# A state-space scan stage: forget-gate sums moved behind a tile's last products, the last output products moved inside the next unit, the last result moved between the forget-gate scans

## The chip, the cores and the metric

The kernel runs on one core of one Trainium2 chip. The metric is the time of one execution on the device in microseconds (us); the value given is the median of several runs. The engines are named as in the profile: PE (TensorE), DVE (VectorE), ACT (ScalarE), POOL (GpSimd) and SP (the queue that issues the weight loads).

## The reference, cut to what matters

The whole computation is a two-block network on one sequence of 512 positions and width 1024, followed by a second block. The second block mixes three branches of the same normalised input: an attention branch, a state-space branch (S5) and a gated linear recurrence (HGRN2). The change touches the S5 branch, the first steps of the HGRN2 branch and the first products of the merge.

```python
# S5: a complex linear recurrence over the 512 positions, 32 groups of 64 states
_, _, h_r, h_i = lax.associative_scan(_complex_linear_combine, elems, axis=1)
y = (jnp.einsum('bsgp,ghp->bsgh', h_r, c_re) - jnp.einsum('bsgp,ghp->bsgh', h_i, c_im))
y = y.reshape(bsz, seq, S5_W) + d_skip * uf
z = jax.nn.gelu(y)
out = z * jax.nn.sigmoid(z @ w_glu + b_glu)

# HGRN2: the log of the forget gate, and its running sum inside a chunk
log_f = jnp.logaddexp(jnp.log(lb), jnp.log1p(-lb) + jax.nn.log_sigmoid(z))
b = jnp.cumsum(lfc, axis=2)

# merge
merged = (gates[:, :, 0] * (y_fox @ wb[:BRANCH_W]) + gates[:, :, 1] * (y_s5 @ wb[BRANCH_W:2 * BRANCH_W])
          + gates[:, :, 2] * (y_hg @ wb[2 * BRANCH_W:]))
```

## The kernel before, in words

Every weight passes through a ring of four slots: SP loads a unit of 128x1024 into `w_stage`, ACT copies its high part to `w_hi`, POOL subtracts to get the low part `w_lo`, and PE multiplies three times for each block (high by high, high by low, low by high, lines 460 to 462). A unit is 24 such products of 128x512.

The S5 stage treats 16 tiles `t` of 128 states. All engines have their own written-out instruction order, and only semaphores tie them. For each tile, PE makes the drive (`drive(t)`, lines 2041 and 2042, into banks 4 and 5). DVE multiplies it by sine and cosine (lines 2130 to 2139, six instructions), scans it along the sequence (lines 2151 and 2153), and makes two products of the imaginary part (lines 2157 and 2158, the tile's last products, semaphore `s5_nprod`). POOL makes two products of the real part (lines 2087 and 2088) and then two additions that join both (line 2092, semaphore `s5_sum`). PE multiplies the sums by the output weights (`outputs(t)`, line 2032, into bank 7, semaphore `s5_ymm`). Since a tile uses the same banks as the one before it, `drive(t)` waits until `s5_nprod` says that the last products of tile `t-1` are made.

Between these steps, PE works through 17 units of other weights: first half of unit `u`, `outputs(u-2)`, second half, `drive(u)`. Units 0 to 11 are projections for HGRN2, whose result DVE takes from the bank (`take`, line 2115), 12 to 15 another projection that ACT takes, and unit 16 is the first of the merge. After unit 16 comes `outputs(15)`, and then the merge goes on in `pe_hg` with the gate `pe_merge_gate(pe, 0, 2, 1)` (the second unit of the merge), a branch (third unit), and the gate of the next triple (fourth unit).

DVE has more work in this loop: `dve_hg_forget_sum` (line 2794) makes for two heads each, in tiles 6 and 8, the log of the forget gate from `hq` and one of `ss` and `hf_odd`. Both operands are in SBUF. `s5_result` (line 2168) takes four tiles' outputs from bank 7; it waits for `s5_ymm`. It runs after tiles 4, 8 and 12, and the fourth time after the loop and after `dve_hg_forget_scan` (line 2801, `ones` and `hq`, both in SBUF; 16 instructions, 4 for each of 4 heads). The fourth result is what ACT's last GELU waits for (line 2242); behind it in ACT's order stand four copies (line 2245) and then `w_hi` of the merge's fourth unit (line 424), which POOL's `w_lo` of that unit (line 455) waits for. DVE goes on with a memset (line 2164), four subtractions for the low part of the GELU (`dve_z`, line 2250, `su` and `y_hi`, both in SBUF) and the scaling of the merge's first gate (line 2296).

The wait of a merge gate on PE names both its weights and its bank:

```python
pe.wait_ge(w_lo_ready, L.base + u + i + 1)
pe.wait_ge(taken, L.rbase + r + i + 1 - RING)
```

For the merge's fourth unit the second line means the first line-2296 instruction: DVE must have taken the first gate from bank 0.

Of the kernel before, what the change touches and what calls it, by code (L numbers as in the profile page):

```python
# [24 lines left out]
KD = D // P  # L25
# [66 lines left out]
def build(nc, io):  # L92
# [1899 lines left out]
    def pe_s5(pe):  # L1992
        QFG, V, M = layers["hg_qfg"], layers["hg_v"], layers["merge01"]

        def first_half(u):
            if u < 12:
                pe.wait_ge(w_lo_ready, QFG.base + u + 1)
                pe.wait_ge(taken, QFG.rbase if u in (1, 2) else QFG.rbase + u + 1 - RING)
            elif u == 16:
                pe.wait_ge(w_lo_ready, M.base + 1)  # L2000
                pe.wait_ge(taken, M.rbase + 1 - RING)
            else:
                pe.wait_ge(w_lo_ready, V.base + u - 12 + 1)
            half(u, 0)

        def half(u, part):

            if 12 <= u < 16:
                k = 2 * (u - 12) + part
                wh, wl = (w[:, u % RING, part * T:(part + 1) * T] for w in (w_hi, w_lo))  # L2010
                for t in range(4):
                    if k == 0:
                        pe.wait_ge(taken, V.rbase)
                    c = slice(t * P, (t + 1) * P)
                    pe.matmul(bank[t][:], xg_hi[:, k, c], wh, start=k == 0, stop=False)
                    pe.matmul(bank[t][:], xg_lo[:, k, c], wh, start=False, stop=False)
                    mm = pe.matmul(bank[t][:], xg_hi[:, k, c], wl, start=False, stop=k == KD - 1)
            else:
                for k in range(4 * part, 4 * part + 4):
                    mm = three_passes(pe, s5_unit_bank(u)[:], u % RING, k, xg_hi[:, k, :], xg_lo[:, k, :], k == 0, k == KD - 1)  # L2020
            if part:
                mm.then_inc(unit_used, 1)

        def outputs(t):

            j = 32 * (t % 4)
            out = bank[7][j:j + 32, :]
            if t >= 4 and t % 4 == 0:
                pe.wait_ge(s5_y, t // 4)
            for c, product in enumerate((gbuf[:], sq[:, 0, :])):  # L2030
                pe.wait_ge(s5_sum, 2 * t + c + 1)
                mm = pe.matmul(out, s5_cx[:, c, t, :], product, start=c == 0, stop=c == 1)  # L2032
            mm.then_inc(s5_ymm, 1)

        def drive(t):
            j, jr = 32 * (t % 4), (32 * (t % 4) + 32) % P
            if t >= 1:
                pe.wait_ge(s5_nprod, 2 * t)
            if t % 4 == 0:
                pe.wait_ge(su_turned, 32 * (t // 4 + 1))  # L2040
            pe.matmul(bank[4][:], s5_bt[j:j + 32, 0, t // 4, :], su[j:j + 32, t // 4, :], start=True, stop=True)  # L2041
            pe.matmul(bank[5][:], s5_bt[jr:jr + 32, 1, t // 4, :], su_r[t // 4 % 2][jr:jr + 32, :],
                      start=True, stop=True).then_inc(s5_drive, 1)

        pe.wait_ge(s5_bt_ready, 2)
        pe.wait_ge(att_exp, FOX_STEPS - 2)
        drive(0)
        pe.wait_ge(s5_turn, 1)
        first_half(0)
        pe_fox_transposes(pe, SLOTS - 1, 0)  # L2050
        pe_fox_outputs(pe, SLOTS - 2)
        pe_fox_transposes(pe, SLOTS - 1, 1)
        half(0, 1)
        pe_fox_outputs(pe, SLOTS - 1)
        pe.wait_ge(s5_cx_ready, 4)
        for u in range(1, 17):
            if u == 3:
                pe.wait_ge(fox_lo, 4)
            first_half(u)
            if u >= 2:  # L2060
                outputs(u - 2)
            half(u, 1)
            if u < 16:
                drive(u)
        outputs(15)

    def s5_unit_bank(u):
        return bank[0 if u == 16 else (u + 2) % RING]
# [41 lines left out]
    def dve_s5(dve):  # L2110
        QFG, V = layers["hg_qfg"], layers["hg_v"]

        def take(t):
            dve.wait_ge(unit_used, QFG.base + t + 1)
            dve.tensor_tensor(hq[:, QFG_TILE[t], :], s5_unit_bank(t)[:], rstd[:], ALU.mult).then_inc(taken, 1)

        for t in range(16):
            if 1 <= t < 12:
                take(t)
            if 1 <= t < 15:  # L2120
                dve_s5_fraction(dve, t + 1)
            if t == 1:
                dve.wait_ge(levels_ready, 1)
            sin, cos, gr = s5_state(t)
            dr, di, m0, m1 = bank[4][:], bank[5][:], s5_m[:, 0, :], s5_m[:, 1, :]
            n0 = 8 * t
            dve.wait_ge(s5_rot, 3 * t + 3)
            dve.wait_ge(s5_drive, t + 1)

            dve.tensor_tensor(m0, dr, sin, ALU.mult).then_inc(s5_step, 1)  # L2130
            dve.tensor_tensor(m1, di, sin, ALU.mult).then_inc(s5_step, 1)
            dve.wait_ge(s5_step, n0 + 1)
            dve.tensor_tensor(dr, dr, cos, ALU.mult).then_inc(s5_step, 1)
            dve.wait_ge(s5_step, n0 + 2)
            dve.tensor_tensor(di, di, cos, ALU.mult).then_inc(s5_step, 1)
            dve.wait_ge(s5_step, n0 + 3)
            dve.tensor_tensor(dr, dr, m1, ALU.add).then_inc(s5_step, 1)
            dve.wait_ge(s5_step, n0 + 4)
            dve.tensor_tensor(di, di, m0, ALU.subtract).then_inc(s5_step, 1)
            if t == 0:  # L2140
                take(0)
                dve_fox_low(dve, 3)
                dve_s5_fraction(dve, 1)
            if t in (6, 8):
                dve_hg_forget_sum(dve, t - 6)
                dve_hg_forget_sum(dve, t - 5)
            mag = s5p[:, 3, t:t + 1].to_broadcast([P, T])
            if t >= 2:
                dve.wait_ge(s5_prod, 2 * t - 2)
            dve.wait_ge(s5_step, n0 + 5)  # L2150
            dve.tensor_tensor_scan(gr, mag, dr, 0.0, ALU.mult, ALU.add).then_inc(s5_step, 1)
            dve.wait_ge(s5_step, n0 + 6)
            dve.tensor_tensor_scan(di, mag, di, 0.0, ALU.mult, ALU.add).then_inc(s5_step, 1)
            if t >= 1:
                dve.wait_ge(s5_sum, 2 * t)
            dve.wait_ge(s5_step, n0 + 8)
            dve.scalar_tensor_tensor(ubuf[:], di, -1.0, sin, ALU.mult, ALU.mult).then_inc(s5_nprod, 1)
            dve.tensor_tensor(sq[:, 1, :], di, cos, ALU.mult).then_inc(s5_nprod, 1)
            if t % 4 == 0 and t:
                s5_result(dve, t // 4 - 1)  # L2160
        for h in range(HEADS):
            dve_hg_forget_scan(dve, h)
        s5_result(dve, 3)
        dve.memset(hsc, 0.0).then_inc(hg_zero, 1)

    def s5_result(dve, i):
# [623 lines left out]
    def dve_hg_forget_sum(dve, h):  # L2790

        dve.wait_ge(hg_key, HEADS)
        dve.wait_ge(hg_ln, h + 1)
        dve.scalar_tensor_tensor(hg_b(h), hg_b(h), 0.0, hg_logf(h), ALU.min, ALU.subtract).then_inc(hg_min, 1)
# [241 lines left out]
            act_merge_gate(act, *unit)  # L3036

    def pe_hg(pe):
        pe_merge_gate(pe, 0, 2, 1)
        pe_merge_branch(pe, 0, 2)  # L3040
        pe_triple(pe, 0, 3)
        pe_glu(pe)
        for h in range(HEADS):
            pe_share(pe, share(h, 0))
            if h:
                pe_hg_out(pe, h - 1)
            pe_hg_scores(pe, h, 0)
            pe_hg_scores(pe, h, 1)
            if h:
                pe_hg_sum(pe, h - 1)  # L3050
            pe_share(pe, share(h, 1))
            pe_hg_scores(pe, h, 2)
            pe_hg_scores(pe, h, 3)
            if h:
                pe_hg_spread(pe, h - 1)
            pe_share(pe, share(h, 2))
            pe_hg_scores(pe, h, 4)
            pe_hg_scores(pe, h, 5)
            pe_share(pe, share(h, 3))
            pe_hg_scores(pe, h, 6)  # L3060
            pe_hg_keys(pe, h)
            pe_hg_scores(pe, h, KD_STEP)
            pe_share(pe, share(h, 4))
            pe_hg_update(pe, h)
        pe_merge_gate(pe, 2, 0, 0, (0, 1, 2, 3, 4))
        pe_hg_out(pe, HEADS - 1)
        pe_merge_gate(pe, 2, 0, 0, (5, 6))
        pe_hg_sum(pe, HEADS - 1)
        pe_merge_gate(pe, 2, 0, 0, (7,))
        pe_merge_gate(pe, 2, 0, 1, (0, 1))  # L3070
        pe_hg_spread(pe, HEADS - 1)
        pe_merge_gate(pe, 2, 0, 1, (2, 3, 4, 5, 6, 7))
# [383 lines left out]
```

## Time and profile before

| | us |
|---|---|
| median of 3 runs (lowest, highest) | 2835.97 (2835.58, 2836.41) |
| the profiled execution: its own time | 2836.24 |
| its span in the trace | 2834.5 |
| PE busy in the span | 2801.3 |

The profiled execution was 0.27 us above the median, and 1.7 us of its time lie around the span. Times of rows count from the span's start. Consecutive DVE instructions overlap a little in the trace: one of 0.69 us is followed by the next after 0.60 us, so that costs are read from start to start.

### The profile page before, as it was taken

To read this page: it belongs to the slowest core of one execution; us is meant where nothing else is said; L and a number is where in the kernel's file an instruction comes from. 1 tells how busy PE (TensorE), PEld (TensorE's weight loads), DVE (VectorE), ACT (ScalarE), POOL (GpSimd) and SP (SyncE) were. 2 spreads that over 40 slices of the span, in tenths; PEclk is the share of its full clock that TensorE was granted. 3 is DMA by queue.
4 is the path that set the end of the run, shared out by engine and by line. 5 is a ranking of instruction groups with operands and counts; after the bars stand their busy time and mean duration, and the time that the engine had idled before them with its cause. 6 is when DMAs were issued, how large, how long until landed. Compare 5 with 4: busy or idle time off the path is not lost.

```text
span 2834.5 us, 45729 instructions
## 1 busy us (share of the span) xinstructions
PE 2801.3 (99%) x16460; PEld 2399.2 (85%) x16460; DVE 1652.0 (58%) x2696; ACT 1346.6 (48%) x2076; POOL 1570.8 (55%) x872
## 2 busy tenths in 40 slices
PE   7999999999999999999999999999999999999999
PEld 6998877899889998888999886765688888799987
DVE  6777147577616774135777416589788363467730
ACT  5554256555525554243555333566444344455531
POOL 5775445677546774443777443158633373377743
PEclk9999999999999999999999999999999999999999
DMA  3223322222332233332223332112222242122332
GB/s 136 104 104 113 104 82 82 90 104 104 104 102 92 104 107 106 99 110 84 90 104 122 99 105 71 48 50 67 82 75 75 97 148 75 52 93 109 111 102 76
DMA packets 80684, 267.89 MB, mean 95 GB/s; under 512 B 11168, under 2 KB 13216, under 8 KB 80560
## 3 DMA queue, kind: packets, MB, share of 16 engines
q1 hardware_dynamic: 77904, 262.01, 27.7%
q10 hardware_dynamic: 2656, 4.26, 0.5%
q8 instruction: 73, 1.20, 0.2%
q14 instruction: 51, 0.42, 0.0%
HBM read 263.09 MB, written 2.10 MB: 94 GB/s over the span
## 4 chain that ended last, share of the span: by engine, by line
PE 93%; DVE 4%; ACT 2%; issue 1%; DMA 0%; POOL 0%; ACTq 0%; SPq 0%; DVEq 0%
PE bank L460 17%; PE bank L461 17%; PE bank L462 17%; PE bank L701 10%; PE bank L703 10%; PE bank L702 10%; PE bank L532 1%; PE bank L534 1%; PE bank L533 1%; PE bank L1620 1%; PE bank L2032 1%; PE bank L2894 1%; PE bank L2630 0%; PE bank L2041 0%; PE bank L2610 0%
## 5 line engine op out<-in xcount | busy, mean ns | idle before, releaser
L448 POOL TENSOR_TENSOR w_lo<-w_stage,w_hi 128x1024 fp32r<-128x1024 f32 (+1 forms) x228 | 533.8, 2347 | 729.8 <-ACT w_hi L424 729.3
L424 ACT ACTIVATE w_hi<-w_stage 128x1024 fp32r<-128x1024 f32 (+1 forms) x412 | 421.1, 1027 | 367.9 <-PE bank L462 301.1
L788 POOL TENSOR_TENSOR w_lo<-w_stage,w_hi 128x1024 fp32r<-128x1024 f32 (+1 forms) x176 | 327.2, 1859 | 201.8 <-ACT w_hi L424 201.8
L460 PE MATMUL bank<-xg_hi,w_hi 128*128 128x512 f32 x976 | 395.9, 406 | 7.9 <-DVE h_raw L1048 6.4
L455 POOL TENSOR_TENSOR w_lo<-w_stage,w_hi 128x1024 fp32r<-128x1024 f32 (+1 forms) x96 | 235.9, 2462 | 263.4 <-ACT w_hi L424 218.9
L461 PE MATMUL bank<-xg_lo,w_hi 128*128 128x512 f32 x976 | 381.1, 390 | 0.0
L462 PE MATMUL bank<-xg_hi,w_lo 128*128 128x512 f32 x976 | 381.0, 390 | 0.0
L460 PE MATMUL bank<-h_hi,w_hi 128*128 128x512 f32 x880 | 342.3, 389 | 0.0
L461 PE MATMUL bank<-h_lo,w_hi 128*128 128x512 f32 x880 | 342.3, 389 | 0.0
L462 PE MATMUL bank<-h_hi,w_lo 128*128 128x512 f32 x880 | 342.3, 389 | 0.0
L703 PE MATMUL bank<-xg_hi,w_lo 128*128 128x256 f32 x1056 | 299.2, 283 | 0.0
L701 PE MATMUL bank<-xg_hi,w_hi 128*128 128x256 f32 x1056 | 298.9, 283 | 0.0
L702 PE MATMUL bank<-xg_lo,w_hi 128*128 128x256 f32 x1056 | 298.8, 283 | 0.0
L701 PE MATMUL bank<-xsum,s_w 128*128 128x256 f32 x1056 | 296.1, 280 | 0.0
L703 PE MATMUL bank<-xsum,s_w 128*128 128x256 f32 x1056 | 294.6, 279 | 0.0
L702 PE MATMUL bank<-xsum,s_w 128*128 128x256 f32 x1056 | 294.6, 279 | 0.0
L1121 DVE SCALAR_TENSOR_TENSOR x_res<-bank,x_res 128x512 f32 x64 | 44.0, 688 | 408.2 <-PE bank L462 408.2
L460 PEld LDWEIGHTS bank<-xg_hi,w_hi 128*128 128x128 f32 x976 | 183.6, 188 | 76.1 <-issue 37.2
L1013 DVE TENSOR_TENSOR s_w<-bank,s_w 128x512 fp32r<-128x512 f32 x176 | 121.7, 692 | 190.3 <-ACT s_w L918 190.3
L461 PEld LDWEIGHTS bank<-xg_lo,w_hi 128*128 128x128 f32 x976 | 183.8, 188 | 40.4 <-issue 4.6
L462 PEld LDWEIGHTS bank<-xg_hi,w_lo 128*128 128x128 f32 x976 | 183.5, 188 | 39.6
L701 PEld LDWEIGHTS bank<-xg_hi,w_hi 128*128 128x128 f32 x1056 | 202.4, 192 | 0.2
(526 smaller groups left out, 6610.5 us busy)
## 6 DMA issues: line engine op xcount, KB each, us to landing
w_stage<-w_up SPq DMA_DIRECT2D x220, 512.0 KB, 4.2
w_stage<-w_down SPq DMA_DIRECT2D x80, 512.0 KB, 3.5
w_stage<-merge SPq DMA_DIRECT2D x36, 512.0 KB, 3.4
w_stage<-w_down SPq DMA_DIRECT2D x40, 384.0 KB, 3.1
w_stage<-hg_qfg SPq DMA_DIRECT2D x12, 512.0 KB, 3.4
w_stage<-rec_r SPq DMA_DIRECT2D x8, 512.0 KB, 3.4
w_stage<-rec_y SPq DMA_DIRECT2D x8, 512.0 KB, 3.5
w_stage<-rec_out SPq DMA_DIRECT2D x8, 512.0 KB, 3.4
```

What stands on the lines that cost most here:

```text
L424: act.activation(w_hi[:, r, 0:w], w_stage[:, r, 0:w], ACT.Copy).then_inc(w_hi_ready, 1)
L448: pool.tensor_tensor(w_lo[:, r, 0:w], w_stage[:, r, 0:w], f32(w_hi[:, r, 0:w]), ALU.subtract).then_inc(w_lo_ready, 1)
L455: pool.tensor_tensor(w_lo[:, r, 0:w], w_stage[:, r, 0:w], f32(w_hi[:, r, 0:w]), ALU.subtract).then_inc(w_lo_ready, 1)
L460: pe.matmul(out, w_hi[:, r, c], hi, start=start, stop=False)
L461: pe.matmul(out, w_hi[:, r, c], lo, start=False, stop=False)
L462: return pe.matmul(out, w_lo[:, r, c], hi, start=False, stop=stop)
L701: pe.matmul(out, wh[:, c], xh[:, k, :], start=k == 0, stop=False)
L702: pe.matmul(out, wh[:, c], xl[:, k, :], start=False, stop=False)
L703: mm = pe.matmul(out, wl[:, c], xh[:, k, :], start=False, stop=k == 3)
L788: pool.tensor_tensor(w_lo[:, r, cs], w_stage[:, r, cs], f32(w_hi[:, r, cs]), ALU.subtract).then_inc(w_lo_ready, 1)
L1013: dve.tensor_tensor(lo, src[:], f32(hi), ALU.subtract).then_inc(wsum_lo_ready, 1)
L1121: dve.scalar_tensor_tensor(tile(x, m), bank[mm % 4][:], scale, tile(x, m), ALU.mult, ALU.add).then_inc(taken, 1)
```

## The change

Three edits. On DVE, the forget-gate sums of tiles 6 and 8 are issued behind that tile's last products instead of ahead of its scans. On PE, the first four of the eight blocks of the gate that follows unit 16 are issued ahead of `outputs(15)` and the other four behind it; the call in `pe_hg` goes. On DVE, the fourth result is issued after the scans of two heads instead of after those of four.

```diff
             if u < 16:
                 drive(u)
+        pe_merge_gate(pe, 0, 2, 1, range(4))
         outputs(15)
+        pe_merge_gate(pe, 0, 2, 1, range(4, KD))
...
-            if t in (6, 8):
-                dve_hg_forget_sum(dve, t - 6)
-                dve_hg_forget_sum(dve, t - 5)
             mag = s5p[:, 3, t:t + 1].to_broadcast([P, T])
...
             dve.tensor_tensor(sq[:, 1, :], di, cos, ALU.mult).then_inc(s5_nprod, 1)
+            if t in (6, 8):
+                dve_hg_forget_sum(dve, t - 6)
+                dve_hg_forget_sum(dve, t - 5)
             if t % 4 == 0 and t:
                 s5_result(dve, t // 4 - 1)
         for h in range(HEADS):
+            if h == 2:
+                s5_result(dve, 3)
             dve_hg_forget_scan(dve, h)
-        s5_result(dve, 3)
         dve.memset(hsc, 0.0).then_inc(hg_zero, 1)
...
     def pe_hg(pe):
-        pe_merge_gate(pe, 0, 2, 1)
         pe_merge_branch(pe, 0, 2)
```

DVE in tile 8, before: the sums (line 2794) stand ahead of the scans (lines 2151 and 2153), and the result (line 2168) follows the last product.

```order
L2139 TENSOR_TENSOR bank<-bank,s_m 128x512
L2794 SCALAR_TENSOR_TENSOR hq<-hq,ss 128x512
L2794 SCALAR_TENSOR_TENSOR hq<-hq,hf_odd 128x512
L2151 SCALAR_TENSOR_TENSOR s_g_136<-s5p,bank 128x512
L2153 SCALAR_TENSOR_TENSOR bank<-s5p,bank 128x512
L2157 SCALAR_TENSOR_TENSOR ubuf<-bank,rot 128x512
L2158 TENSOR_TENSOR sq<-bank,rot 128x512
L2168 SCALAR_TENSOR_TENSOR su<-su,par,bank 128x512
L2115 TENSOR_TENSOR hq<-bank,rstd 128x512
```

The same stretch of DVE in the changed kernel (its line 2797 is the sum, 2171 the result, 2117 the take):

```order
L2141 TENSOR_TENSOR bank<-bank,s_m 128x512
L2150 SCALAR_TENSOR_TENSOR s_g_136<-s5p,bank 128x512
L2152 SCALAR_TENSOR_TENSOR bank<-s5p,bank 128x512
L2156 SCALAR_TENSOR_TENSOR ubuf<-bank,rot 128x512
L2157 TENSOR_TENSOR sq<-bank,rot 128x512
L2797 SCALAR_TENSOR_TENSOR hq<-hq,ss 128x512
L2797 SCALAR_TENSOR_TENSOR hq<-hq,hf_odd 128x512
L2171 SCALAR_TENSOR_TENSOR su<-su,par,bank 128x512
L2117 TENSOR_TENSOR hq<-bank,rstd 128x512
```

The two sums now stand behind the tile's last product, directly ahead of the result and the take; tile 6 is the same without the result.

DVE behind the last tile in the changed kernel (line 2804 is the forget-gate scan, 2253 the subtraction of `dve_z`, 2299 the scaling of the gates):

```order
L2157 TENSOR_TENSOR sq<-bank,rot 128x512
L2804 SCALAR_TENSOR_TENSOR hq<-ones,hq 128x128 x8
L2171 SCALAR_TENSOR_TENSOR su<-su,par,bank 128x512
L2804 SCALAR_TENSOR_TENSOR hq<-ones,hq 128x128 x8
L2167 MEMSET sq 128x512
L2253 TENSOR_TENSOR y_lo<-su,y_hi 128x512 x4
L2299 TENSOR_TENSOR gbuf<-bank,rstd 128x512
```

Before, all 16 scans stood ahead of the result. Eight of them moved behind it.

## Rows read from the trace of the kernel before

**Rows 1.** The page: busy time of each engine over the span.

```profile
PE 2801.3 (99%) x16460; PEld 2399.2 (85%) x16460; DVE 1652.0 (58%) x2696; ACT 1346.6 (48%) x2076; POOL 1570.8 (55%) x872
```

**Rows 2.** Waits of PE from 1860 to 2100 us: total, times, longest.

```profile
PE bank L2041 <- DVE sq L2158: 2.1, 3, 1.0
PE bank L2032 <- POOL gbuf L2092: 1.2, 1, 1.2
PE bank L460 <- POOL w_lo L455: 1.2, 1, 1.2
```

**Rows 3.** Timeline of DVE, tiles 6 to 8: start, duration, instruction.

```profile
1919.21 0.69 DVE L2130 TENSOR_TENSOR s_m<-bank,rot 128x512 f32<-128x512 f32 x1
...
1922.81 0.68 DVE L2794 SCALAR_TENSOR_TENSOR hq<-hq,ss 128x512 f32<-128x512 f32 x1
...
1924.01 1.21 DVE L2151 TENSOR_TENSOR_SCAN s_g<-s5p,bank 128x512 f32<-128x512 f32 x1
...
1927.65 0.68 DVE L2115 TENSOR_TENSOR hq<-bank,rstd 128x512 f32<-128x512 f32 x1
...
1929.03 0.69 DVE L2130 TENSOR_TENSOR s_m<-bank,rot 128x512 f32<-128x512 f32 x1
...
1946.37 0.74 DVE L2168 SCALAR_TENSOR_TENSOR su<-su,par,bank 128x512 f32<-128x512 f32 x1
1947.03 0.68 DVE L2115 TENSOR_TENSOR hq<-bank,rstd 128x512 f32<-128x512 f32 x1
```

**Rows 4.** Timeline of PE: the drives of tiles 7, 8 and 10.

```profile
1927.79 0.69 PE L2041 MATMUL bank<-su,s_bt 32*128 32x512 f32 x1 [0.91 <-DVE sq L2158]
...
1936.63 0.69 PE L2041 MATMUL bank<-su,s_bt 32*128 32x512 f32 x1
...
1955.59 0.69 PE L2041 MATMUL bank<-su,s_bt 32*128 32x512 f32 x1 [0.18 <-DVE sq L2158]
```

**Rows 5.** Timeline of POOL in tile 6.

```profile
1920.47 2.41 POOL L455 TENSOR_TENSOR w_lo<-w_stage,w_hi 128x1024 fp32r<-128x1024 f32 x1
1925.30 1.30 POOL L2087 TENSOR_TENSOR gbuf<-s_g,rot 128x512 f32<-128x512 f32 x1 [2.42 <-DVE s_g L2151]
1926.55 1.28 POOL L2088 TENSOR_TENSOR sq<-s_g,rot 128x512 f32<-128x512 f32 x1
1927.79 1.27 POOL L2092 TENSOR_TENSOR gbuf<-gbuf,ubuf 128x512 f32<-128x512 f32 x1
```

**Rows 6.** Line 2801 and line 2454: duration min/median/max, first and last start.

```profile
L2801 DVE TENSOR_TENSOR_SCAN hq<-ones,hq x16: 393/394/2522, 2008.2 to 2017.2; 128x128 f32<-128x128 f32 x16
...
L2454 DVE SCALAR_TENSOR_TENSOR m_lo<-merged,m_hi x8: 678/2873/2878, 2286.7 to 2300.4; 128x512 fp32r<-128x512 f32 x8
```

**Rows 7.** Timelines of DVE and POOL behind the last tile.

```profile
2008.19 0.47 DVE L2801 TENSOR_TENSOR_SCAN hq<-ones,hq 128x128 f32<-128x128 f32 x1
2008.59 1.41 DVE L2801 TENSOR_TENSOR_SCAN hq<-ones,hq 128x128 f32<-128x128 f32 x1
...
2008.34 1.38 POOL L2092 TENSOR_TENSOR gbuf<-gbuf,ubuf 128x512 f32<-128x512 f32 x1
...
2011.02 2.49 POOL L455 TENSOR_TENSOR w_lo<-w_stage,w_hi 128x1024 fp32r<-128x1024 f32 x1
```

**Rows 8.** Scans of line 2801 in one stretch: length, DVE busy (count), clock, DMA.

```profile
2013.60:2017.50 3.90, 3.90 (x13) 1.00 0.19 69
```

**Rows 9.** Timelines of DVE, POOL and PE, from the fourth result to the merge's fourth unit.

```profile
2017.49 0.72 DVE L2168 SCALAR_TENSOR_TENSOR su<-su,par,bank 128x512 f32<-128x512 f32 x1
...
2019.43 2.50 DVE L2250 TENSOR_TENSOR y_lo<-su,y_hi 128x512 fp32r<-128x512 f32 x4 [0.68 <-ACT y_hi L2245]
2021.85 0.68 DVE L2296 TENSOR_TENSOR gbuf<-bank,rstd 128x512 f32<-128x512 f32 x1
...
2021.99 2.38 POOL L455 TENSOR_TENSOR w_lo<-w_stage,w_hi 128x1024 fp32r<-128x1024 f32 x1 [8.49 <-ACT w_hi L424]
...
2012.09 0.50 PE L460 MATMUL bank<-xg_hi,w_hi 128*128 128x512 f32 x1
...
2024.43 0.50 PE L460 MATMUL bank<-xg_hi,w_hi 128*128 128x512 f32 x1 [1.17 <-POOL w_lo L455]
```

## The prediction, made before the changed kernel ran

> **What bounds the kernel now.** I read the page first: PE is busy in 2801.3 of 2834.5 us [rows 1], so that only what PE waits for, some 33 us in all, can be gained. Then I read PE's waits in the stretch that the change touches. There are three kinds: three waits of drives for a tile's last products on DVE, 2.1 us together, one wait of the last output products for POOL's sums, 1.2 us, and one of the merge's fourth unit for its low weights, 1.2 us [rows 2]. The change aims at all of them, and all of them together are 4.5 us, 0.16% of the time. 0.2% of it, 5.7 us, is about what a measurement of this kernel can tell from no change. So the first answer is that even a full success is hardly measurable; the rest of the text asks for the sign.
>
> The timelines then show how tight the loop is. From the drive of tile 7 to that of tile 8 PE takes 8.84 us with no wait [rows 4]. DVE's part of this round is: the first multiplication starts 1.24 us after the drive (1927.79 to 1929.03) [rows 3, 4]; from there to the end of the last product are 7.24 us (1919.21 to 1927.65, less 1.20 for the two sums that lie between) [rows 3]; PE follows that end by 0.14 us (1927.65 to 1927.79) [rows 3, 4]. Together 8.62, so a tile has 0.22 us to spare, and whatever DVE is given in addition comes out as a wait of a drive, whether it stands ahead of the scans or behind the products. Position changes only what it meets.
>
> **The sums.** Two instructions in tile 6 and two in tile 8. Where they stand now, each pair costs 1.20 us (1922.81 to 1924.01) [rows 3]. POOL is idle in that time: its `w_lo` ends at 1922.9 and its next product waits for DVE's scan until 1925.30 [rows 5]. Behind the products it is different. Without the sums ahead of the scans, POOL's second product runs from 1925.35, and its first sum begins at 1926.59 (1926.55 and 1927.79, less 1.20) [rows 5], and POOL goes on without a pause for two sums and a `w_lo`. DVE's last product ends at 1926.45. So the moved pair falls between POOL instructions that stand back to back.
>
> What this costs I read where it already happens, behind tile 15, where the scans of line 2801 take the very place that the sums get. The first is issued 0.15 us ahead of POOL's sum at 2008.34 and passes; the second is issued at 2008.59 and lasts 1.41 us, as long as POOL's instruction, in place of the usual 0.39 [rows 6, 7]. The longest is 2.52 us, beside a `w_lo` of 2.49 [rows 6, 7]. Line 2454, a 128x512 instruction of the sum's form with both inputs in SBUF, has a median of 2.87 us where it runs beside `w_lo` and 0.68 at least [rows 6]. The instructions of the S5 tile itself, which have one input in PSUM, are not stretched beside the same POOL instructions (0.69 and 0.68 in tile 6 to 8) [rows 3]. I read: one DVE instruction with two SBUF inputs passes between two of POOL's, and the next waits one whole POOL instruction.
>
> The Trainium skill says this of the port pair that VectorE and GpSimd share (SBUF — State Buffer, Who interferes with whom): a VectorE instruction with two SBUF inputs and a GpSimd instruction that reads SBUF exclude each other, and the later one blocks until the earlier is done. By that rule the moved sums lose time; by the sums' own rows alone (0.68 each) they would win a little. The trace agrees with the rule, with 0.39 against 1.41 us.
>
> Tile 6 by that: the first sum waits from 1926.45 to 1926.59 and takes about 0.5; POOL's sum, 1.25 us, goes ahead of the second, until 1928.35; the second ends at 1928.85. Take and the next fraction are 1.20 (two at 0.60), the first multiplication of tile 7 starts at 1930.05, its last product ends 7.24 later at 1937.29, and drive 8 starts at 1937.43, against 1936.63 before [rows 4]: 0.80 later. (PE would be free for it at about 1935.7: 1927.79 less the wait of 0.91, and 8.84 [rows 4].) Tile 8: the first multiplication at 1938.67, last product 1945.91, drive 9 without a wait at 1946.27. The pair costs 2.40 again, to 1948.31, and now the result of 0.66 us (1946.37 to 1947.03) [rows 3] stands behind it, to 1948.97; take and fraction 1.20, 1950.17; last product 1957.41, drive 10 at 1957.55 against 1955.59 [rows 4]. From there on the rounds are as before. **Sums: 1.95 us lost.** Bounds: 0.45 gained if nothing collides (the same chain with 1.20 in place of 2.40 gives drive 10 at 1955.14, since DVE's short pause ahead of the take is used), 4.5 lost if each pair meets one more POOL instruction of 1.25. I take the middle, since the phase of 0.14 us is that of tile 15, which has been seen.
>
> **The end of the stage**, in times of the trace before, without the shift of 1.95. PE has no wait behind unit 16: 12 products, at 0.23 us each 2.8 us ((2024.43 less 1.17 less 2012.09) by 48) [rows 9], run while POOL makes the sums. The wait of 1.2 for the first sum, and one of 0.3 for the second, go. The weights and the bank of that gate are ready, since POOL's `w_lo` of this unit is made two instructions ahead of the products of tile 15. The output products end at about 2013.4 in place of 2012.1. The second half of the gate follows, and PE wants the fourth unit at 2024.43 less the waits of 1.17, 1.2 and 0.3, which is 2021.8.
>
> Does it get it? The scans go through at one to each POOL instruction until the `w_lo` of 2011.02 is over; the other 12 take 3.90 us, 0.325 each (the row counts one of the waiting ones too) [rows 7, 8]. So the first eight are done at 2017.49 less 2.6, 2014.9, behind the output products: the result starts there with no wait and 2.6 us earlier than now. ACT and then POOL follow as before 4.50 us after it (2017.49 to 2021.99) [rows 9]: `w_lo` at 2019.4, its own 2.4, ready at 2021.8. That is just in time.
>
> But the fourth unit also needs the first gate taken. DVE is behind the result at 2015.55, behind the other scans at 2018.15, behind the memset at 2018.75 (result to line 2250 is 1.94 with a wait of 0.68 in it, so 0.6 for the memset) [rows 9]. Now the four line-2250 subtractions start, 0.605 each [rows 9], both inputs in SBUF, and POOL's `w_lo` falls at 2019.4 into the middle of them; before, it started at 2021.99, 0.14 us after the last [rows 9]. It holds DVE up by some 2.3 us. Line 2296 starts at 2023.4 in place of 2021.85, ends at 2024.1, and PE starts the fourth unit at 2024.15, against 2024.43. **End of the stage: 0.3 us gained.** Bounds: nothing if DVE is held for 2.6 us, 2.5 gained if the subtractions are not held (line 2296 at 2021.2, PE at 2021.9). I take the collision, since both starts follow from chains seen in the rows and they fall well inside each other.
>
> From there on PE has nothing to wait for until DVE's work on the scores, which itself starts when PE ends the next branch; DVE idles twice for over 4 us before it, so that lateness of a microsecond on DVE or ACT is absorbed, and the shift is carried to the end.
>
> **The sum.** 1.95 less 0.3 is 1.65 us lost. The profiled execution would go from 2836.24 to 2837.9; the median from 2835.97 to 2837.6.
>
> **Rivals.**
> *No collisions.* DVE and POOL do not hold each other in the new places: sums gain 0.45, the end gains 2.5, the time is 2833.0. For it speaks only that the sums are 0.68 us long now; against it the stretched rows [rows 6]. 10%. Only the sums free, the subtractions held: 2835.2, 4%.
> *The sums collide, the subtractions don't* (ACT's chain is later, or POOL waits): 1.95 less 2.5, the time is 2835.4. 12%.
> *Slower: the sums miss the gap.* The first sum passes only because DVE asks 0.14 us ahead of POOL's sum. If DVE's last product ends more than 0.14 us later relative to POOL, each pair meets two POOL sums and costs 1.25 more, twice: 2.5, the time is 2840.1. Tile 15 shows the gap met once, which speaks against. 8%.
> *The wait at the new result.* If the output products ended later than 2014.9, DVE's other scans would stand behind the wait; each 1 us beyond would be 1 us at the fourth unit. By the rows there are 1.5 us to spare. 3%.
>
> **How the numbers follow.** The forecast of 2837.6 has 63%; its own range is 2836.6 to 2838.6, from the 0.1 to 0.3 us that each of the four collisions is uncertain. The range of 2834.0 to 2839.5 adds the second rival and the half-collision and the smaller forms of the others, and leaves out the first and the third. All cases are within 0.2% of 2835.97 (2830.3 to 2841.6), so "same" has 95%; 2% and 3% are left for what I have not seen on either side.
>
> **What the changed profile would show.** Line 2797: two short and two long ones, 1.4 to 1.9 us, in place of four at 0.68. Drives: 8 and 10 wait, 1.8 and 2.4 us, 7 and 9 don't. No wait at line 2032 for POOL. The result starts 6.7 us after DVE's last product in place of 9.3. One line-2253 subtraction of 2.5 to 3 us. At the merge's fourth unit a wait of some 2.4 us for line 2299 and not for `w_lo`. I am wrong if line 2797 stays at 0.68, or if PE's waits in this stretch sum to less than 4.5 us.

## The result and the profile after

The changed kernel is slower: median 2845.71 us (2837.16 to 2849.76, 7 runs) against 2835.83 (2832.78 to 2838.14, 7 runs), ratio 1.0033, 95% interval 1.0024 to 1.0043. The forecast was 1.65 us more; it is nearly 10. The profiled execution took 2849.76 us with a span of 2847.9.

The steps that were forecast are there, at their places and nearly at their sizes. PE's waits over the whole span of the changed kernel, longest sums first (total, times, longest):

```profile
PE bank L486 <- ACT xg_hi L3244: 8.3, 1, 8.3
PE bank L460 <- DVE h_raw L1048: 4.3, 1, 4.3
PE bank L2041 <- DVE sq L2157: 4.0, 2, 2.3
PE bank L460 <- DVE yh_lo L1267: 2.7, 6, 0.8
PE bank L460 <- DVE gbuf L2299: 2.5, 1, 2.5
```

The drives' waits are 4.0 us in place of 2.1, the wait of the output products for POOL is gone, and the merge's fourth unit waits 2.5 us for line 2299 and no longer 1.2 for its low weights [rows 2]. Within the touched stretch this is 6.5 us of waits in place of 4.8 (0.3 of the second sum with it), 1.7 us more, which is what the prediction had.

The moved sums, DVE and POOL in tile 6 of the changed kernel (timelines: start, duration, instruction):

```profile
1928.54 0.68 DVE L2157 TENSOR_TENSOR sq<-bank,rot 128x512 f32<-128x512 f32 x1
1929.14 0.76 DVE L2797 SCALAR_TENSOR_TENSOR hq<-hq,ss 128x512 f32<-128x512 f32 x1
1929.82 1.75 DVE L2797 SCALAR_TENSOR_TENSOR hq<-hq,hf_odd 128x512 f32<-128x512 f32 x1
1931.50 0.68 DVE L2117 TENSOR_TENSOR hq<-bank,rstd 128x512 f32<-128x512 f32 x1
...
1928.04 1.31 POOL L2090 TENSOR_TENSOR sq<-s_g,rot 128x512 f32<-128x512 f32 x1
1929.30 1.73 POOL L2094 TENSOR_TENSOR gbuf<-gbuf,ubuf 128x512 f32<-128x512 f32 x1
1930.99 1.74 POOL L2094 TENSOR_TENSOR sq<-sq 128x512 f32<-128x512 f32 x1
```

The first sum passes between two POOL instructions, the second waits for one. The pair takes 2.36 us (1929.14 to 1931.50) where it took 1.20 [rows 3]. POOL pays as well: its sums take 1.73 us where one took 1.27 [rows 5], since each stands behind a DVE instruction. This agrees with the Trainium skill on the shared port (SBUF — State Buffer, Who interferes with whom). The rows also give the order: in each of these three cases the instruction that waits goes next.

The drives of tiles 8 and 10, on PE:

```profile
1940.06 0.69 PE L2041 MATMUL bank<-su,s_bt 32*128 32x512 f32 x1 [1.69 <-DVE sq L2157]
...
1960.12 1.01 PE L2041 MATMUL bank<-su,s_bt 32*128 32x512 f32 x1 [2.35 <-DVE sq L2157]
```

They wait 1.69 and 2.35 us; 1.8 and 2.4 were forecast. But the second one is 1.01 us long where it was 0.69 [rows 4]. That is the first sign of what was not forecast. The end of the stage, on DVE and POOL:

```profile
2022.66 0.71 DVE L2171 SCALAR_TENSOR_TENSOR su<-su,par,bank 128x512 f32<-128x512 f32 x1
2023.30 2.62 DVE L2804 TENSOR_TENSOR_SCAN hq<-ones,hq 128x128 f32<-128x128 f32 x8
2025.98 0.48 DVE L2167 MEMSET sq<- 128x512 f32 x1
2026.38 4.61 DVE L2253 TENSOR_TENSOR y_lo<-su,y_hi 128x512 fp32r<-128x512 f32 x4
2030.91 0.68 DVE L2299 TENSOR_TENSOR gbuf<-bank,rstd 128x512 f32<-128x512 f32 x1
...
2027.16 2.69 POOL L455 TENSOR_TENSOR w_lo<-w_stage,w_hi 128x1024 fp32r<-128x1024 f32 x1 [5.96 <-ACT w_hi L424]
```

The four subtractions take 4.61 us where they took 2.50 [rows 9], because the low weights now fall into them. PE starts the merge's fourth unit at 2031.74, with a wait of 2.50. From DVE's end of tile 15 that is 15.9 us (2015.85 to 2031.74), where it was 16.2 (2008.19 to 2024.43) [rows 7, 9]: 0.35 gained, 0.3 forecast.

So where are the other 8 us? The page gives PE 2816.7 us busy in place of 2801.3 [rows 1], with the same instructions: PE did the same work more slowly. (The profiled execution is 13.5 us longer than that of before: 15.4 us of slower work and the 1.7 us of waits, less 3.3 us by which the first two waits of the kernel, 8.3 and 4.3 us here, are shorter than before's 9.5 and 6.4, at the start and far from the change, and 0.3 us elsewhere.) Stretches around the wait of drive 10, around that of the fourth unit, and one ahead of the whole change (stretch: length, busy and count of PE, PEld, DVE, ACT and POOL, then granted clock, DMA share and GB/s):

```profile
1957.00:1958.00 1.00, 0.77 (x4) 0.29 (x2) 1.00 (x2) 0.81 (x1) 0.37 (x1) 1.00 0.74 225
1958.00:1960.00 2.00, 0.00 (x0) 0.00 (x0) 1.90 (x4) 0.00 (x0) 2.00 (x2) 1.00 0.14 49
1960.00:1961.00 1.00, 0.89 (x4) 0.31 (x4) 1.00 (x3) 0.00 (x0) 1.00 (x2) 0.68 0.00 0
1961.00:1967.00 6.00, 6.00 (x16) 3.80 (x12) 5.15 (x9) 4.52 (x7) 3.91 (x3) 0.50 0.16 53
1967.00:1968.00 1.00, 1.00 (x3) 0.25 (x3) 1.00 (x1) 0.00 (x0) 0.00 (x0) 0.91 0.54 217
...
2030.00:2031.00 1.00, 0.00 (x0) 0.00 (x0) 1.00 (x3) 0.00 (x0) 0.00 (x0) 1.00 0.07 18
2031.00:2032.00 1.00, 0.26 (x1) 0.29 (x2) 1.00 (x2) 0.37 (x1) 0.00 (x0) 1.00 0.72 227
2032.00:2035.00 3.00, 3.00 (x8) 2.30 (x8) 2.12 (x4) 2.98 (x5) 1.72 (x1) 0.51 0.02 5
...
1759.00:1769.00 10.00, 10.00 (x29) 6.22 (x26) 5.13 (x14) 3.61 (x10) 2.37 (x2) 0.50 0.05 7
```

Right behind each of the two long pauses the granted clock falls from 2.4 to 1.2 GHz, 0.50 in the column, for some 6.8 and 3.4 us. Sixteen products are made in six microseconds where the kernel before, at the full clock, makes 22 or 23 behind the same drive. The third stretch, 10 us at half clock, ends 160 us ahead of the first instruction that the change moved, behind a pause of only 0.46. Two more, near 2271 and 2441 us, follow no long pause either. The trace of before has none between 50 and 2800 us. Half clock behind 50 us costs this execution 15.4 us in all, 5.1 of them behind the two long pauses and 10.2 at the three other places. One trace each doesn't tell what of this the change did; that was the question for the experiments.

### The profile page after: what moved, and what is told of

The parts are those of the page before. It is cut to its first block, busy times and chain, and to the rows that moved or that the text cites. A ratio compares the mean times of both kernels' runs of the same rounds, so it can differ in the third digit from the quotient of the medians.

```text
span 2847.9 us, 45729 instructions
## 1 busy us (share of the span) xinstructions
PE 2816.7 (99%) x16460; PEld 2411.0 (85%) x16460; DVE 1650.1 (58%) x2696; ACT 1348.8 (47%) x2076; POOL 1572.5 (55%) x872
## 4 chain that ended last, share of the span: by engine, by line
PE 92%; DVE 4%; ACT 2%; issue 1%; DMA 0%; ACTq 0%; SPq 0%; DVEq 0%
PE bank L460 17%; PE bank L461 17%; PE bank L462 17%; PE bank L701 10%; PE bank L703 10%; PE bank L702 10%; PE bank L532 1%; PE bank L534 1%; PE bank L533 1%; PE bank L1620 1%; PE bank L2032 1%; PE bank L2897 1%; PE bank L2041 1%; PE bank L2633 0%; PE bank L2613 0%
## 5 line engine op out<-in xcount | busy, mean ns | idle before, releaser
L788 POOL TENSOR_TENSOR w_lo<-w_stage,w_hi 128x1024 fp32r<-128x1024 f32 (+1 forms) x176 | 327.4, 1860 | 203.2 <-ACT w_hi L424 202.9
```

Source lines behind the costliest of these rows:

```text
L788: pool.tensor_tensor(w_lo[:, r, cs], w_stage[:, r, cs], f32(w_hi[:, r, cs]), ALU.subtract).then_inc(w_lo_ready, 1)
```

## The experiments

Each execution comes with its time and its mean granted clock, the latter to three decimals, which alone leaves 1.4 us open in one execution; so means are compared. Two numbers are used: the mean time, and the mean of time times clock, which takes out what the clock cost and leaves work and waits. (If the clock is low while PE pauses anyway, that product takes out a little too much.) The mean time of the changed kernel is uncertain by 0.8 us (one standard error), of the filled ones together by 0.4, of the single runs by 0.4 to 1.5; time times clock by 0.2 to 0.6.

| kernel | executions | mean us | mean clock | time times clock |
|---|---|---|---|---|
| before (on four chips together) | 122 | 2836.2 | 0.9981 | 2830.8 |
| before, run as `control` | 11 | 2835.4 | 0.9985 | 2831.0 |
| changed (first runs, `after_rep`, `after_rep2`) | 30 | 2843.1 | 0.9959 | 2831.6 |
| `sums_only` | 11 | 2839.9 | 0.9976 | 2833.2 |
| `end_only` | 12 | 2838.5 | 0.9969 | 2829.7 |
| `pause2` | 11 | 2839.1 | 0.9976 | 2832.4 |
| `pause4` | 11 | 2842.3 | 0.9968 | 2833.3 |
| `pause8` | 8 | 2844.5 | 0.9969 | 2835.6 |
| `pause8_fill` | 6 | 2844.5 | 0.9972 | 2836.5 |
| `after_fill`, `after_fill2` | 22 | 2838.5 | 0.9978 | 2832.1 |
| `after_zlate` | 12 | 2838.7 | 0.9967 | 2829.2 |
| `end_zlate`, `end_zlate2` | 22 | 2833.9 | 0.9979 | 2828.0 |
| `best` | 11 | 2836.2 | 0.9972 | 2828.2 |

Before's clock was 0.9978 on the chip on which `control`, `sums_only`, `end_only` and `pause4` ran, and 0.9981 to 0.9982 on the three others; against before on their own chip the four took 1.5 us less and 3.0, 1.6 and 5.4 us more.

Two theories stood against each other: P, that the long pauses of PE bring the stretches at half clock, and R, that these belong to the chip or the hour.

**Is the clock the chip's?** The kernel before, run as a kernel of its own.

> The kernel before, unchanged, run as if it were a new one, so that the granted clock of each of its executions is listed. Theory P (the PE pauses that the change made longer bring stretches at half clock): clock 0.998 to 0.999 in nearly all executions, time 2836, no stretch at half clock behind 50 us. Rival R (the stretches belong to the chip or the hour, not to the change, since one of them lies ahead of the first changed instruction): clock 0.993 to 0.998 here too, and single executions up to 2845.

Measured: median 2834.87, ratio 0.9995 (0.9986 to 1.0003), clock 0.997 at the lowest, none of the 11 executions at 0.996 or below; of the changed kernel's 30 it is 20. But its trace isn't clean: it has half-clock time too, near 2260 and 2428 us, 1.7 us lost at each. The first as a stretch of ten microseconds (same columns):

```profile
2260.00:2270.00 10.00, 10.00 (x75) 10.00 (x75) 1.27 (x3) 7.08 (x10) 5.91 (x3) 0.85 0.16 54
```

So such stretches occur in the kernel before as well, a few us an execution, at places that have nothing to do with the change. R holds for those and not, by these 11 executions, for the whole difference.

**The two halves of the change.** First the sums alone behind the products.

```diff
-            if t in (6, 8):
-                dve_hg_forget_sum(dve, t - 6)
-                dve_hg_forget_sum(dve, t - 5)
             mag = s5p[:, 3, t:t + 1].to_broadcast([P, T])
...
+            if t in (6, 8):
+                dve_hg_forget_sum(dve, t - 6)
+                dve_hg_forget_sum(dve, t - 5)
```

> Only the forget-gate sums are moved behind the last products. The waits alone: drives 8 and 10 wait 1.7 and 2.35 us, and the time is 1.9 us longer than before, 2837.7. Theory P: a stretch at half clock of 3 to 7 us behind the wait of 2.35 us in most executions, which costs 1.7 to 3.4 us more, so 2839 to 2841, clock 0.997. Rival R: 2837.7 and a clock as the control's. If the whole clock loss of the changed kernel came from the sums: 2844.

Measured: ratio 1.0011 (1.0002 to 1.0019). The drives wait 4.0 us as in the changed kernel, and the second sums last 1.755 us. Time times clock is 2.4 us above before's; 1.95 was forecast for the waits. No half-clock stretch followed the wait of 2.3 us in its trace, and its clock is as before's within the spread. This run speaks for R.

Then the end of the stage alone: the gate's first half ahead of `outputs(15)` and the result between the scans.

```diff
+        pe_merge_gate(pe, 0, 2, 1, range(4))
         outputs(15)
+        pe_merge_gate(pe, 0, 2, 1, range(4, KD))
...
+            if h == 2:
+                s5_result(dve, 3)
             dve_hg_forget_scan(dve, h)
```

> The sums stay ahead of the scans; the gate's first half goes ahead of the last output products, and the fourth result between the forget-gate scans. The waits alone: one wait of 2.5 us at the merge's fourth unit in place of three of 1.2, 0.3 and 1.2, 0.3 us gained, 2835.5. Theory P: a stretch at half clock behind it, 2837 to 2839. Rival R: 2835.5.

Measured: ratio 1.0006 (0.9997 to 1.0015). The waits are those forecast, and time times clock falls by 1.1 us, more than the 0.3 forecast. The time rises nonetheless: behind the 2.5 us wait the clock is at half. Stretches of this kernel:

```profile
2024.00:2026.00 2.00, 0.17 (x1) 0.00 (x0) 2.00 (x3) 0.00 (x0) 0.77 (x1) 1.00 0.05 9
2026.00:2028.00 2.00, 1.33 (x6) 1.08 (x7) 1.81 (x3) 1.44 (x2) 0.00 (x0) 0.96 0.33 122
2028.00:2030.00 2.00, 2.00 (x6) 1.62 (x5) 1.31 (x2) 1.98 (x4) 1.78 (x1) 0.50 0.00 0
```

Five of its 12 executions have a clock of 0.996 or less, of before's 122 it is 3 in 100. This speaks for P.

**A pause alone.** Nothing of the change; DVE repeats one multiplication of tile 9, so that drive 10 waits longer. `n` is 2, 4 or 8.

```diff
+            for _ in range(n if t == 9 else 0):
+                dve_chain(dve, dve.tensor_tensor(m0, dr, sin, ALU.mult))
             dve.tensor_tensor(m0, dr, sin, ALU.mult).then_inc(s5_step, 1)
```

> The kernel before with four repeats of one multiplication (same inputs, same output) in tile 9 ahead of the real one: nothing moved, only the wait of drive 10 becomes some 2.6 us long (4 times 0.61 to 0.66 and the 0.2 it has). The waits alone: 2.5 us more, 2838.4. Theory P: a stretch at half clock behind that wait, 2840 to 2842, clock 0.997, and possibly others later. Rival R: 2838.4, clock as the control's.

> Two repeats: the wait of drive 10 is some 1.6 us. Time times clock 2832. Theory P with a pause that is too short for it (no trace so far has a stretch right behind a pause of 1.8 us or less): clock as before's, time 2837.

> The kernel before with eight repeats of one multiplication in tile 9 in place of four: the wait of drive 10 is some 5.5 us. With the clock's losses taken out, time times mean clock: 2.5 us above the four repeats' 2833.2, so 2836. Theory P: a stretch at half clock right behind the wait in the trace, and a mean clock below before's by 0.001 to 0.002. Rival R: clock as before's.

Measured: ratios 1.0012 (1.0003 to 1.0021), 1.0020 (1.0010 to 1.0030) and 1.0031 (1.0020 to 1.0041) for 2, 4 and 8 repeats, with longest waits of 1.6, 3.0 and 6.0 us. Time times clock rises by 1.6, 2.5 and 4.8 us. The clock is 0.9976, 0.9968 and 0.9969, against before's 0.9982, 0.9978 and 0.9982 on the same chips. The time grows by 2.9, 6.1 and 8.3 us, the wait of drive 10 by 1.4, 2.9 and 5.8, which leaves 1.5, 3.2 and 2.5 us beyond the wait. So the short pause, too, came out slower than its wait, against the expectation, though no half clock follows it in its trace. In the traces the clock falls behind the waits of 3.0 and 6.0 us and not behind that of 1.6. In the longest, it falls while PE still waits (stretches of `pause8`):

```profile
1954.00:1956.00 2.00, 0.00 (x0) 0.00 (x0) 2.00 (x3) 0.00 (x0) 0.00 (x0) 0.71 0.00 0
1956.00:1957.00 1.00, 0.00 (x0) 0.00 (x0) 1.00 (x2) 0.00 (x0) 0.78 (x1) 0.50 0.00 0
```

In that trace the clock is at half from 1954.85 to 1965.09, and 3.9 us of that lie in the wait, where they cost PE nothing. That fits eight repeats losing no more time beyond the wait than four; it rests on one trace.

**The same pause, filled.** `pause8` with 18 idle products on PE while drive 10 waits, whose results are overwritten.

```diff
+            if u == 10:
+                pe.wait_ge(w_lo_ready, QFG.base + u + 2)
+                pe.wait_ge(taken, QFG.rbase + u + 2 - RING)
+                for _ in range(6):
+                    three_passes(pe, s5_unit_bank(u + 1)[:], (u + 1) % RING, 0, xg_hi[:, 0, :], xg_lo[:, 0, :], True, True)
             if u < 16:
                 drive(u)
```

> The same eight repeats, and PE makes 18 idle products (a later block's, whose results are overwritten) while it would wait for drive 10, so that its pause is about 1.3 us and the drive no later. Time times clock as without them, 2836. Theory P: no stretch at half clock behind drive 10, and a mean clock as before's, so 2 to 5 us less than without the idle products. Rival R: no difference.

Measured: ratio 1.0032 (1.0019 to 1.0044), the same time as without the filling. Its trace has no half clock behind drive 10, but stretches near 2265 and 2435 us. Theory P had 2 to 5 us less. With 6 executions against 8 and an uncertainty of 1.0 us in each mean, this pair speaks against P and doesn't decide.

**The changed kernel, its pauses filled.** Nine idle products ahead of drive 10 (the lines above with 3 in place of 6), and nine ahead of the fourth unit:

```diff
+        pe.wait_ge(w_hi_ready, layers["merge01"].base + 4)
+        for _ in range(9):
+            pe.matmul(bank[4][:], w_hi[:, 3, 0:P], xg_hi[:, 0, :], start=True, stop=True)
         pe_triple(pe, 0, 3)
```

> The changed kernel again, beside the others. Time times mean granted clock, which takes the clock's losses out of a time, was 2831.1 for it and 2830.7 for before. Theory P: the clock is lower than before's by 0.003, and the time 8 to 10 us longer, as in its first seven executions. Rival R (the first seven met a poor chip or hour): clock as before's, time 1 to 2 us longer. By the two single parts so far, whose clocks were 0.0002 and 0.0009 below before's, neither holds in full: the sum would be 0.0011, some 5 us with the waits.

> The changed kernel with 9 idle products ahead of drive 10 and 9 ahead of the merge's fourth unit, in the waits of 2.35 and 2.5 us, so that PE pauses 0.3 to 0.6 us there. The waits on the way stay, so time times clock is the changed kernel's, 2831.5. Theory P: the clock of before, and so 3 to 6 us less than the changed kernel. Rival R: as the changed kernel.

> The changed kernel once more, on the same chip as the next two. So far 2845.3 and 2842.4 us in the mean of 7 and 12 executions, mean clock 0.9950 and 0.9962. If the difference to the kernel with idle products was one of chips, it comes out at 2838 here; by theory P at 2841 or more, clock 0.996 or less.

> The changed kernel with the idle products in its two long waits, on the same chip as the changed kernel itself. Theory P: 3 to 5 us less in the mean, mean clock higher by 0.001 to 0.002, time times clock the same within 1 us. Rival R: no difference.

Measured: the changed kernel again 1.0024 (1.0014 to 1.0033) and 1.0025 (1.0013 to 1.0036), filled 1.0007 (0.9998 to 1.0016) and 1.0011 (1.0002 to 1.0020). The last two of each ran on one chip: 2842.6 against 2838.4 us in the mean of 11 executions each, clock 0.9962 against 0.9978. Time times clock is the same, 2831.8 and 2832.2: the way is as long, only the clock differs. More work on PE makes this kernel 4.2 us faster, with a standard error of 1.6; all 30 executions against all 22 give 4.7, with one of 0.9. On the changed kernel (`after_rep2`), and then with the pauses filled (`after_fill2`), the same two stretches:

```profile
1950.00:1960.00 10.00, 7.68 (x19) 4.39 (x18) 8.84 (x14) 4.91 (x8) 7.29 (x5) 0.66 0.21 66
...
2020.00:2030.00 10.00, 7.50 (x26) 5.77 (x25) 9.12 (x9) 4.33 (x5) 6.56 (x3) 0.83 0.15 46
```

```profile
1950.00:1960.00 10.00, 9.73 (x38) 5.68 (x37) 9.79 (x14) 6.10 (x9) 7.38 (x5) 1.00 0.20 72
...
2020.00:2030.00 10.00, 9.52 (x43) 7.58 (x42) 9.12 (x11) 4.90 (x6) 5.67 (x3) 1.00 0.16 52
```

**The second pause taken away.** The changed kernel with the first two gates scaled ahead of the four subtractions, whose first result PE needs only at 2043.0 in this trace, 10 us after the last of them ends; the collision then delays nothing that PE waits for.

```diff
-        dve_z(dve)
         dve_hg(dve)
...
-        dve_triple(dve, 0, 2)
+        dve_merge_gate(dve, 0, 2, 0)
+        dve_merge_gate(dve, 0, 2, 1)
+        dve_z(dve)
+        dve_merge_branch(dve, 0, 2)
```

> The changed kernel, with the scaling of the first merge gates ahead of the four subtractions that collided with the low weights. The wait of 2.5 us at the merge's fourth unit goes. Waits alone: 2.2 us less than the changed kernel. Theory P: the stretch at half clock that followed that wait goes too, 4 to 6 us less than the changed kernel. Rival R: 2.2 us less.

> The same, with the sums ahead of the scans as in the kernel before. No wait at the fourth unit, three waits gone: 2.5 us less than before with the clock's losses taken out, and in theory P a clock at or above before's, so 2.5 to 4 us less in the time. If the port collision is not what delayed the first gate, the wait of 2.5 us stays.

> The second part with the gates scaled ahead of the subtractions, sums as before: 3.2 us less than before with the clock taken out, on the last job, but its clock was 0.0008 lower and the time only 0.8 less. If that clock was chance, 2 to 3 us less than before now; if a program with fewer waits gets a poorer clock too, 0 to 1.

Measured for the first: ratio 1.0009 (1.0000 to 1.0018), 4.5 us less than the changed kernel in the mean, of which 2.4 are the wait (time times clock) and the rest the clock. Against `after_rep` on the same chip it is 3.7, between the two theories (4 to 6 and 2.2). For the other two, which have the sums ahead of the scans: ratios 0.9997 (0.9989 to 1.0006) and 0.9990 (0.9981 to 0.9999), in the mean of 22 executions 2833.9, 2.3 us less than before, and 2.8 less in time times clock, 2.5 forecast. PE's waits in that stretch of `end_zlate2`:

```profile
PE bank L2041 <- DVE sq L2160: 2.1, 3, 1.0
PE bank L460 <- POOL w_lo L455: 0.4, 1, 0.4
```

So the second and third edits are good ones once the line-2299 scaling goes ahead. It is the only version that came out faster than the kernel before, and by no more than 0.1%; of its two runs only the second is clear of no change. Three executions of the first have a clock of 0.996, without a wait of more than 1.0 us there.

**The sums one by one.** The kernel of the last two runs, with each sum alone behind the products of tiles 6, 7, 13 and 14.

```diff
+            if t in (6, 7, 13, 14):
+                dve_hg_forget_sum(dve, (6, 7, 13, 14).index(t))
```

> As the last one, with the four sums singly behind the last products of tiles 6, 7, 13 and 14. One instruction passes between two of POOL's, so each should last 0.76 and none 1.75 us; behind tiles 13 and 14 DVE idles for 0.9 us and more, so two are free; the waits of drives fall from 2.1 to about 0.7 us. With the clock's losses taken out 4 us less than before; the time 4 to 5 us less.

Measured: ratio 1.0003 (0.9994 to 1.0012). Each sum lasts 0.74 to 0.75 us, as expected: alone, it passes. But the drives still wait 2.0 us, and my expectation of 0.7 was wrong, as was that of the time: 2.6 us less than before with the clock taken out, for 4 forecast, and no less in the time, for 4 to 5. One drive waits 1.80, for a DVE that waited itself:

```profile
1944.48 0.69 DVE L2110 SCALAR_TENSOR_TENSOR frac<-turn,bank 128x512 f32<-128x512 f32 x1 [1.53 <-ACT turn L2195]
```

ACT had stood 4.3 us at the next forget gate (line 2782, `hf_odd`), whose buffer the second sum frees, and that sum now came one tile later:

```profile
1933.37 0.63 ACT L2782 ACTIVATE hf_odd<-hq 128x512 f32<-128x512 f32 x1 [4.31 <-DVE hq L2796]
```

What I had priced on DVE and POOL went to ACT.

## Why the prediction was wrong

- **The sums**: right. 1.95 us lost was forecast. In the traces, drive 10 comes 1.84 us later counted from the take of tile 6 (1920.65 to 1960.12, before 1917.96 to 1955.59), and `sums_only` gave 2.4 with the clock taken out. The pair's cost of 2.40 measured 2.36. The rivals of no collision and of the missed gap are out: two sums lasted 0.76 and two 1.75.
- **The end of the stage**: right in each step; 0.35 us gained in the trace against 0.3. The result starts 6.8 us after DVE's last product (6.7 forecast, 9.3 before). Alone, with the clock taken out, it gave 1.1. The wait at the new result did not occur.
- **"From there on PE has nothing to wait for", "the shift is carried to the end"**: right for the waits; time times clock is up by 0.8 us, with a standard error of 0.3, under the 1.65 of the sum. Why it is less was not found.
- **The step that failed** is that of the sum itself: it costed each pause of PE by its own length. The last part of the prediction lists waits of 1.8, 2.4 and 2.4 us, in a kernel whose longest in that stretch had been 1.2 [rows 2], and nothing in the working asked what such pauses do to PE's clock. A clock that falls behind a pause was in no term, no rival and no bound, so the upper end of 2839.5 lay below six of the first seven executions and 23 of all 30, and "all cases are within 0.2%" was false. What the runs showed in its place: of 7.0 us by which the changed kernel is slower in the mean (30 executions against 122), 0.8 are waits and work and 6.1 are clock. Filling its two long pauses with idle products gave back 4.2 us (standard error 1.6) of the 6.7 that it was slower than before on one chip, and raised the clock from 0.9962 to 0.9978, nearly before's 0.9981.
- **What stays open.** Not every long pause did it. Over the traces and behind 50 us, 11 waits of 2.3 us or more occurred in kernels that leave them empty; 8 were followed or met by half clock and 3 were not (both in `after_rep`, one in `sums_only`). Each of the 17 traces also has a wait of 3.0 to 6.5 us near 35 to 43 us, before's too (line 460, for `h_raw`); 13 were followed or met by half clock, and 4 of 3.0 to 3.2 us were not. `sums_only` has such a pause and lost no clock worth the name, `after_zlate` has the same one and has 0.9967; with 11 and 12 executions I can't say whether that is chance. And half-clock stretches without a long pause come and go: near 2265 us in every trace but that of before, near 2435 in 8 of the 17, near 1760 in 5 (`after`, `after_rep`, `after_zlate`, `end_only` and `pause4`). In the three traces of the changed kernel, half clock cost 5.1, 0 and 5.1 us at the two long pauses and 10.2, 6.8 and 5.1 us at those other places; in the two filled ones 1.7 us each, all at the other places. So the traces have more of it away from the pauses than at them, and why the other places should be worse in the changed kernel, if they are, was not found. That empty pauses cost clock is shown by filling them and by `pause4` and `pause8`; how the 6.1 us divide between the two pauses and the other places is not shown.

## What to carry to other kernels

When a change makes one pause of the matmul engine longer, cost it by its length and by the clock behind it: here a pause of some 2.4 us cost about 2 us more than itself on average (an estimate: half of the 4.2 us that filling two of them gave back), and `sums_only`, which has one, showed nothing of it in its clock. No half clock followed the ten waits of 1.6 to 1.9 us, so two short waits may be better than one long one of the same sum; that was not tried, and the short pause of `pause2` was not free either. And an instruction with two SBUF inputs on VectorE is cheap where GpSimd pauses (0.68 us here), passes singly between two GpSimd instructions (0.74 to 0.76), and waits for a whole GpSimd instruction when it is the second of a pair (1.75); before moving one, look at what the other engine does in the new place, and at who waits for the buffer that it frees.

## What was not expected of the hardware

- The granted clock fell to half at or behind 7 of 10 waits of 2.3 to 3.0 us, in stretches of 3.4 to 6.8 us, and in the wait of 6.0 us, for 10.2; of ten waits of 1.6 to 1.9 us in these traces none was followed by it. Of the waits near 35 us, the four shortest, of 3.0 to 3.2 us, were not followed by it, and the 13 of 3.4 to 6.5 us were, or had it fall within them.
- It also fell in stretches without a long pause, for example for 10 us after 1759 us in the changed kernel, behind a pause of 0.46 us, and near 2260 us in the unchanged kernel's `control` trace.
- Idle products made the changed kernel faster by 4.2 us on one chip (standard error 1.6), with time times clock unchanged (2831.8 and 2832.2); in `pause8` they gave nothing.
- Where a moved sum met POOL's additions, the instruction that waited went next each time: POOL's additions grew from 1.27 to 1.73 us, DVE's second sum from 0.68 to 1.75.
